# Second FFN output GEMM of a decoder layer with the tokens stationary, in two passes, and its norm per token tile

## The reference

```python
def swiglu(u, w_in, w_out):
    a, b = jnp.split(u @ w_in, 2, axis=-1)
    return (jax.nn.silu(a) * b) @ w_out
...
    h = swiglu(modulate(x, 2), p['w_ffn2_in'], p['w_ffn2_out'])
    x = layer_norm(ALPHA * x + 0.5 * gate[:, 2] * h, p['ln_gain'][2], p['ln_bias'][2])
```

## Time and profile before

| | us |
|---|---|
| median of 3 runs (lowest, highest) | 1374.67 (1374.25, 1376.31) |
| the profiled execution, its own time | 1382.03 |
| span of its trace | 1380.3 |
| mean granted clock of PE over the span | 0.967 |
| PE busy | 1300.8 |
| DVE busy | 564.1 |
| ACT busy | 425.6 |
| POOL busy | 183.5 |

### The profile page before, as it was taken

The page is one execution under the profiler, slowest core; times in us unless marked ns, Lnnn a source line. Parts: engine busy times, 40 slices in busy tenths (PEclk is TensorE's granted clock), DMA queues, the critical chain, the costliest instruction groups (busy, mean ns, idle before and its releaser), DMA issues.

```text
span 1380.3 us, 26475 instructions
## 1 busy us (share of the span) xinstructions
PE 1300.8 (94%) x10178; PEld 1199.9 (87%) x10178; DVE 564.1 (41%) x964; ACT 425.6 (31%) x678; POOL 183.5 (13%) x351
## 2 busy tenths in 40 slices
PE   4999999999999997998979899979999999999996
PEld 3899999999999997996646667979999999999995
DVE  2423222232233357115458766673333233323355
ACT  2222222222211225225446654243222222211123
POOL 3000000000000024552280061032000000000020
PEclk8899999999999998999989999979999999999996
DMA  9544545455444343863740063212222322222211
GB/s 296 162 135 146 158 122 174 130 151 153 132 133 134 109 104 77 194 148 88 229 115 3 2 193 100 82 41 77 84 83 76 91 76 85 78 71 84 84 56 69
DMA packets 253198, 156.08 MB, mean 113 GB/s; under 512 B 46187, under 2 KB 247159, under 8 KB 253063
## 3 DMA queue, kind: packets, MB, share of 16 engines
q1 hardware_dynamic: 247759, 139.83, 36.2%
q0 software_dynamic: 5376, 15.43, 3.8%
HBM read 150.86 MB, written 8.60 MB: 116 GB/s over the span
## 4 chain that ended last, share of the span: by engine, by line
PE 85%; DVE 7%; ACT 4%; issue 2%; DVEq 1%; DMA 1%; SPq 0%; POOL 0%; POOLq 0%; ACTq 0%
PE ps L307 69%; PE ps L776 3%; PE ps L1968 2%; PE ps L785 1%; PE ps L1162 1%; PE ps L284 1%; ACT AR L1383 1%; DVE AR L2001 1%; DVE XT L470 1%; PE ps L1179 1%; PE ps L369 1%; DVEq L469 1%; PE ps L1270 1%; DMA AR<-in_x_sample_dram 1%; DVE UL L353 1%
## 5 line engine op out<-in xcount | busy, mean ns | idle before, releaser
L267 DVE TENSOR_TENSOR WL<-RAW,WH 128x1024 fp32r<-128x1024 f32 x159 | 197.2, 1241 | 408.9 <-ACT WH L263 403.6
L307 PE MATMUL ps<-UH,WH 128*128 128x288 f32 x1680 | 359.9, 295 | 3.1 <-ACT MU L641 1.6
L307 PE MATMUL ps<-UL,WH 128*128 128x288 f32 x1680 | 359.3, 294 | 0.0
L307 PE MATMUL ps<-UH,WL 128*128 128x288 f32 x1680 | 357.9, 294 | 0.0
L307 PEld LDWEIGHTS ps<-UH,WH 128*128 128x128 f32 x1680 | 268.4, 188 | 3.6 <-ACT MU L641 1.8
L307 PEld LDWEIGHTS ps<-UH,WL 128*128 128x128 f32 x1680 | 269.9, 188 | 0.0
L307 PEld LDWEIGHTS ps<-UL,WH 128*128 128x128 f32 x1680 | 268.7, 188 | 0.0
L263 ACT ACTIVATE WH<-RAW 128x1024 fp32r<-128x1024 f32 x159 | 167.2, 1052 | 212.2 <-PE ps L307 202.8
L307 PE MATMUL ps<-HH,WH 128*128 128x288 f32 x704 | 152.6, 298 | 2.9 <-DVE HL L658 2.7
L506 POOL TENSOR_TENSOR AR<-AR 128x576 f32<-128x576 f32 x18 | 29.5, 1640 | 940.3 <-ACT AR L417 877.1
L307 PE MATMUL ps<-HH,WL 128*128 128x288 f32 x704 | 150.8, 295 | 0.0
(11 more groups left out here) (307 smaller groups left out, 1279.1 us busy)
## 6 DMA issues: line engine op xcount, KB each, us to landing
RAW<-in_w_ffn_in_dram SPq DMA_DIRECT2D x88, 512.0 KB, 4.9
AW<-in_w_ada_dram SPq DMA_DIRECT2D x56, 512.0 KB, 4.4
RAW<-in_w_ffn_out_dram SPq DMA_DIRECT2D x32, 448.0 KB, 3.7
RAW<-in_w_ffn_out_dram SPq DMA_DIRECT2D x16, 512.0 KB, 4.0
AR<-in_w_ada_dram SPq DMA_DIRECT2D x7, 1024.0 KB, 10.8
RAW<-in_w_in_dram SPq DMA_DIRECT2D x28, 256.0 KB, 4.0
AR<-in_cache_k_cmp_dram POOLq DMA_DIRECT2D x64, 64.0 KB, 2.6
AR<-in_cache_k_slc_dram SPq DMA_DIRECT2D x64, 64.0 KB, 3.2
```

Of the source, the lines that this page charges most:

```text
L267: nc.vector.tensor_tensor(WL[:, slot, :], RAW[:, slot, :], WH[:, slot, :].bitcast(F32), ALU.subtract).then_inc(split_done, 1)
L307: mm = nc.tensor.matmul(ps[:, 2 * uslot + h, 0:HT], W[:, wslot, k * P:(k + 1) * P], R[:, k0 + k, h * HT:(h + 1) * HT], start=(first and k ...
```

## The change

The output GEMM of the second FFN now has the hidden activations as the stationary operand and the weights as the moving one, so its result has tokens on partitions. The first FFN stays as it was.

- A chunk is one contraction tile, 128 full rows of `w_ffn2_out` (4 KB a row). There are 22, and each is loaded and split twice, once per pass over the tokens: `tokens_sp`, `tokens_hi`, `tokens_lo`, 44 chunks. A third load buffer is used, `AW[:, 1]`.
- The tokens are five units: prompt tiles 0 to 3 of 128 tokens and the 64 sample tokens (unit 4). The first pass does units 0, 4 and 1, the second 2 and 3. A prompt unit takes six matmuls of 512 columns per chunk (three products by two halves of the features), the sample unit four: its high and low parts lie beside each other in `H2` and form one stationary tile of 128, whose two halves of the result are added at the end (`PAIR`).
- In the first pass PE also transposes x from `XT` to rows (`turn_x`, nine fills after chunks 2, 4, ... 18); ACT writes them times ALPHA to `XA`.
- At the pass's last chunk (21) and at the last two (42 and 43) the matmuls go unit by unit. Chunk 42 has none of its own: they are issued with those of chunk 43.
- A unit's norm is along the free axis: DVE multiplies by the gate (`gated`), adds x and sums (`summed`), ACT squares with the mean as bias and sums (`squares_at`) and takes the root, DVE forms `(x + nmean) * gain` (`scaled`) and `* rstd + bias` (`shifted`). For units 0, 1 and 4 this stands between the splits of the second pass, for 2 and 3 at the end. The last steps of unit 2 are shared by ACT, DVE and POOL.
- Gate, gain and bias rows are spread over the partitions by 23 DMAs of POOL at the start of the first pass; the gate row is transposed in the input GEMM (`gate_rows_pe`, `gate_rows_act`) and written to DRAM first.
- The old residual, sums, broadcasts, transposes and copies of the last norm go. SP stores eight pieces instead of ten, the first three before the end.

The core of the diff:

```diff
 PHASES = [("setup", 0, 4, 4), ("ffn1_in", 2 * FT, FT, FT), ("ffn1_out", 3 * KT, 4, 4), ("ln0", 0, 1, 0),
           ("w_in", 15, 8, 7), ("w_out", 8, 4, 4), ("ln1", 0, 1, 0), ("ffn2_in", 2 * FT, FT, FT),
-          ("ffn2_out", 3 * KT, 4, 4), ("ln2", 0, 1, 0), ("y", 0, 3, 2)]
+          ("ffn2_out", 2 * FT, 0, 0)]
...
+        def tokens_sp(sp, w2):
+            n0 = CH0["ffn2_out"]
+            for j in range(2 * FT):
+                dst, full, _count = raw_at(j)
+                sp.wait_ge(split_done, n0 + j + 1 if j < 2 else n0 + j)
+                k = j % FT
+                sp.dma_start(dst, w2[0, k * P:(k + 1) * P, :]).then_inc(full, 16)
+
+        def tokens_hi(act, j):
+            n = CH0["ffn2_out"] + j
+            src, full, count = raw_at(j)
+            act.wait_ge(full, count)
+            if j - 2 == FT - 1:
+                act.wait_ge(tok_mm, len(EARLY))
+            else:
+                act.wait_ge(chunk_mm, n + 1 if j - 2 < FT - 1 else n)
+            nc.scalar.activation(WH[:, n % 2, :], src, ACT.Copy).then_inc(hi_done, 1)
...
+            def part(j, t, q):
+                k, w = j % FT, (n0 + j) % 2
+                W = (WH, WH, WL)[q]
+                if t == 4 and q == 1:
+                    return None
+                if q == 2:
+                    pe.wait_ge(split_done, n0 + j + 3)
+                at = TP if t == 4 else t * P + (T + TS if q == 1 else 0)
+                src = H2[:, k, at:at + P]
+                for h in range(2):
+                    out = ps[:, OBANK[t][h] if t < 4 else h, :]
+                    mm = nc.tensor.matmul(out, src, W[:, w, h * 512:(h + 1) * 512], start=(k == 0 and q == 0),
+                                          stop=(k == FT - 1 and q == 2))
+                return mm
...
+            for j in range(2 * FT):
+                k, units = j % FT, (EARLY, LATE)[j // FT]
+                pe.wait_ge(hi_done, n0 + j + 1)
+                if j < FT:
+                    pe.wait_ge(hl_done, FT + 2 + k)
...
+                if j < 2 * FT - 2 and k < FT - 1:
+                    for q in range(3):
+                        for t in units:
...
+                            mm = part(j, t, q)
+                    mm.then_inc(chunk_mm, 1)
+                elif k == FT - 1 and j < FT:
...
+                elif k == FT - 1:
+                    for t in units:
+                        for c in (j - 1, j):
+                            for q in range(3):
+                                mm = part(c, t, q)
+                        mm.then_inc(tok_mm, 1)
...
+        def tokens_dve(dve):
...
+            gated(dve, 3)
+            summed(dve, 3)
+            for h in range(2):
+                gated(dve, 4, h)
+            rstd_at(dve, 3, 4)
+            nc.vector.tensor_tensor(NMR, NMT[:, 2:3], RST[:, 2:3], ALU.mult).then_inc(nmr_ready, 1)
+            summed(dve, 4)
+            nc.vector.drain()
+            scaled(nc.vector, 4)
+            rstd_at(dve, 4, 5)
+            for h in range(2):
+                shifted(nc.vector, 4, h)
+            dve.wait_ge(xn_done, 1)
+            nc.vector.tensor_tensor(y2(1), y2(1), b2("gain", 1), ALU.mult)
+            nc.vector.drain()
+            nc.vector.tensor_tensor(y2(1), y2(1), b2("bias", 1), ALU.add).then_inc(y_done, 1)
```

More of the change, by code:

```diff
@@ L472, in ln_dve @@
                         center(m + 2)
-                if mod is not None and m >= 1:
+                if m >= 1:
                     mod_lo(dve, m - 1, mod)
@@ L479, in ln_act @@
             nc.scalar.activation(SDV, VAR, ACT.Sqrt, bias=EPSC[0:TT, :]).then_inc(sd_ready, 1)
-            if mod is not None:
-                hi(act, *split_args(AFTER[mod], 1))
+            hi(act, *split_args(AFTER[mod], 1))
             for m in range(KT):
                 act.wait_ge(normed, KT * i + m + 1)
[L484 to L491, removed]
                 if m >= 2:
@@ L559, in in_body @@
                         first_pair(pe, a, KT * 3)
+                    if i == 2 and first and j == 1:
+                        gate_rows_pe(pe)
                     if i == 1:
@@ L691, in ffn_dve @@
             dve.sem_inc(stat_in, 1)
[L692 removed]
+            it, q = KT // 2 - 1, 0
             for j in range(6):
@@ new lines, in build @@
+        OBANK = {0: (4, 5), 1: (6, 7), 4: (4, 4), 2: (2, 3), 3: (0, 1)}
+        XA = AR2[:, 0:KT * T]
+        BC = carve(AR2[:, KT * T:AR2N], KT * T, [("gate", D), ("gain", D), ("bias", D), ("gate_s", 512), ("gain_s", 512),
+                                                 ("bias_s", 512)])
+        GROWS = nc.dram_tensor("gate_rows_dram", [NC, D], F32, kind="Internal").ap()
+        NMT, SUMT, SQT, SDT, RST = (MU[:, 8 * q:8 * q + 5] for q in range(5))
+        NMR = MU[:, 40:41]
+        TMP = T2[:, :, :].rearrange("p a n -> p (a n)")
@@ new lines, in gated @@
+        def gated(dve, u, h=None):
+            t = UNITS[u]
+            n = 2 if t < 4 else 1
+            if not h:
+                nc.vector.drain()
+            if u != 1:
+                dve.wait_ge(tok_mm, u + 1)
+            out, src, g = (TMP[:, 0:n * 512].rearrange("p (h n) -> p h n", h=n), obanks(t),
+                           spread_row("gate", t).rearrange("p (h n) -> p h n", h=n))
+            if h is not None:
+                out, src, g = out[:, h], src[:, h], g[:, h]
+            nc.vector.tensor_tensor(out, src, g, ALU.mult).then_inc(tok_read, 1)
@@ new lines, in summed, with mean_at @@
+        def summed(dve, u):
+            t = UNITS[u]
+            nc.vector.drain()
+            x = unit(XA, t)
+            z = nc.vector.tensor_tensor_reduce(out=x, in0=TMP[:, 0:x.shape[1]], in1=x, scale=1.0, scalar=0.0, op0=ALU.add, op1=ALU.add,
+                                               accum_out=SUMT[:, t:t + 1])
+            if t == 4:
+                z.then_inc(sum_s, 1)
+                return
+            nc.vector.drain()
+            mean_at(u, SUMT[:, t:t + 1])
+        def mean_at(u, src):
+            t = UNITS[u]
+            nc.vector.tensor_scalar(NMT[:, t:t + 1], src, -1.0 / D, None, ALU.mult).then_inc(nm_ready, 1)
@@ new lines, in rstd_at, with quarters, ytile, scaled @@
+        def rstd_at(dve, u, count):
+            t = UNITS[u]
+            dve.wait_ge(sdt_ready, count)
+            nc.vector.reciprocal(RST[:, t:t + 1], SDT[:, t:t + 1])
+            nc.vector.drain()
+        def quarters(ap):
+            return ap.rearrange("p (k n) -> p k n", n=256)
+        def ytile(t):
+            if t not in (2, 3):
+                return quarters(unit(XA, t))
+            return early_columns(4 * (t - 1))
+        def scaled(eng, u):
+            t = UNITS[u]
+            eng.scalar_tensor_tensor(out=ytile(t), in0=quarters(unit(XA, t)), scalar=NMT[:, t:t + 1],
+                                     in1=quarters(spread_row("gain", t)), op0=ALU.add, op1=ALU.mult)
@@ new lines, in shifted, with y2, b2 @@
+        def shifted(eng, u, h=None):
+            t = UNITS[u]
+            x, b = ytile(t), quarters(spread_row("bias", t))
+            if h is not None:
+                x, b = x[:, 2 * h:2 * h + 2, :], b[:, 2 * h:2 * h + 2, :]
+            eng.scalar_tensor_tensor(out=x, in0=x, scalar=RST[:, t:t + 1], in1=b, op0=ALU.mult,
+                                     op1=ALU.add).then_inc(y_done, 1)
+        def y2(h):
+            return ytile(2)[:, 2 * h:2 * h + 2, :]
+        def b2(name, h):
+            return quarters(BC[name])[:, 2 * h:2 * h + 2, :]
@@ L756, in build, with tail_pool @@
+        def tail_pool(pool):
+            pool.wait_ge(xn_done, 1)
+            nc.gpsimd.tensor_tensor(y2(0), y2(0), b2("gain", 0), ALU.mult)
+            pool.drain()
+            nc.gpsimd.tensor_tensor(y2(0), y2(0), b2("bias", 0), ALU.add).then_inc(y_pool, 1)
         wav = w_ada[0].rearrange("(k p) n -> p k n", p=P)
```

318 lines of the change are left out of this document (232 added, 86 removed).

## The result

| | before | changed |
|---|---|---|
| median, us (lowest, highest; 8 runs each) | 1376.07 (1374.18, 1380.81) | 1368.08 (1364.85, 1371.37) |
| profiled execution, its own time | 1382.03 | 1366.22 |
| span of its trace | 1380.3 | 1364.6 |
| from one pace behind the last input matmul's start, to the end of the last output matmul | 146.9 | 152.7 |
| from there to the span's end | 28.75 | 13.1 |

The ratio of the times is 0.993, with a 95% interval of 0.9913 to 0.9947: faster by 9.6 us (7.3 to 12.0). The forecast was 17.2, and 1357.5 us for the time (1354 to 1361, over its cases 1350.5 to 1365): the median of 1368.1 lies outside.

The account below looks back on a forecast made before the run. TensorE, busy 94% of the span, and the serial tail behind it were taken as the bound; 0.8 us from the GEMM plus 16.45 from the tail, 17.2 off 1374.67, gave 1357.5 (1354 to 1361; over the cases 1350.5 to 1365).

Parts of the forecast that it names:

- the size of a wide matmul: Output GEMM of the second FFN: 616 matmuls of 512 columns at 225 ns each, 138.6 us (131.4 to 144.1).
- the upper bound of 234: Output GEMM: a 512-column matmul's time if the whole 131.7 ns of a 288-column one scales with the columns.
- the plain float32 row: Profile row of 14 plain float32 matmuls, read as 255 ns each, 15 over 240; taken to set excess per matmul.
- Rival (a): Output GEMM: no excess on a wide matmul, 216 ns each, TensorE ends 5.6 us earlier, 1351.9 us; chance 0.14.
- The small matmuls: Output GEMM: 32 transposes 3.8, 8 plain half-width matmuls 0.6, pair sums 0.6, together 5.0 us; 1.0 more unplaced.
- The stall: Output GEMM, before the last two chunks: TensorE waits 1.35 us for chunk 43's high part, with no lower clock charged.
- The wait of 2.69 us and the clock behind it: Start of the output GEMM: TensorE's wait for the last HL piece and the lower clock after it both go.
- The tail: After TensorE's last matmul: 12.3 us to the end instead of 28.75, a gain of 16.45.
- is hidden: Tail: GpSimd's half of tile 2's gain and bias, 2 x 1.06 us from T + 3.9, claimed to be covered.
- (b): Second pass: norm work between splits makes TensorE wait, 1 us at each of seven insertions, 1364.5 us; chance 0.13.
- (c): Second-pass weight loads set the pace and the kernel gets slower, 1415 us at a landing of 10.8; chance 0.05.

## Why the prediction was wrong, and where it was right

**The failed step is the size of a wide matmul.** "I take 213.3 + 11.7 = 225 ns" put the excess on the matmul. It goes with the columns: 233.4 ns at 512, at the upper bound of 234 that the prediction had worked out and not taken. This is 616 x 8.4 ns = 5.2 us of the 7.6 that the gain fell short.

The argument for it was the plain float32 row, 255 ns apart for 240 of columns, so "the excess goes with the matmul". That row was misread. Its 14 starts include two that came late; the nine behind them are even (timeline of the kernel before, window 806.6 to 812):

```profile
806.41 2.35 PE L1298 MATMUL ps<-AR 128*128 128x288 f32 x9
```

(2.35 - 0.41)/8 = 242.5 ns, where the columns streamed twice are 240: 2.5 over, and not 15. At the same width the reduced type has 12.2 over its 120. Read so, the row speaks against a cost of each matmul and shows the excess to be the type's own.

The runs show, for this type, 0.456 to 0.460 ns a column at three widths (with one exception, the 0.443 at half width), the same with zero activations, and next to none of the excess with 2-byte parts. At 1.2 GHz rows 3 show none with 4-byte parts either (240 ns for 288 columns), and the prediction had read that as a per-matmul cost that hides. A limit of some 0.45 ns a column explains both this (0.833 a column there) and the plain float32 row (0.842), which are slower anyway. That last step is an argument; no run changed the clock, and the 0.443 says that such a limit would not be a fixed number.

Seen this way the new GEMM had to lose: it streams 315,392 columns instead of 304,128, 3.7% more at nearly one price per column. Rival (a) would have been true of 2-byte parts, and is the wrong side of the truth here.

**The small matmuls: 5.0 + 1.0 against 7.3.** The 32 transposes came out near their price, 3.5 for 3.8. The sample's fill, the join of its halves and its sums took 3.3 instead of 1.2. The trace has two records for each plain float32 matmul (the join is two matmuls in the program and x4 in the rows above, L1298 is 8 and x16), so the "8 of 512 columns in 1.92 us" were four matmuls, and fill and join were priced at half. Besides, the two halves of the fill ran mostly one behind the other (16 records from 1225.95 to 1227.26), and the four matmuls of the sums (0.6) had no term.

**The stall: 1.35 forecast, 1.46 measured**, in the place named, and taken out by the experiment with a buffer of its own. The clock stayed at 1.00 through it, as assumed.

**The wait of 2.69 us and the clock behind it: right.** Both are gone, and alone they are worth 4.5 us of GEMM (4.2 forecast).

**The tail: 12.3 forecast, 13.1 measured.** The steps came within some 0.3 us, most on the short side, but for the two beside GpSimd. The prediction allowed 0.3 for them from rows 9; they took 0.74 and 1.06 longer than alone (0.3 of the first is covered: without it VectorE waits 0.29 for the root), and the experiment without GpSimd brings the tail to 12.3. That this is the forecast's number is luck: VectorE does two operations more there than the forecast had, and the last store needs less than the changed kernel's. It also shows that "is hidden" was true of the end of GpSimd's half and not of its effect.

**Rivals (b) and (c)** did not come about: the second pass has no wait but the one, and a load lands in 3.4 us. With 2-byte parts one chunk, the last, waited for its load.

**The sum.** Gains: tail 15.65, wait and clock 4.35. Losses: 4.2 for more columns (143.8 against 1056 x 0.1322 = 139.6), 1.6 for stall and drains, and 4.3 for small matmuls (7.3 now, where the sums between the products and what could not be placed made 2.95). 20.0 - 10.1 = 9.9 by the traces, 9.6 by the times.

## What to carry to other kernels

Price a matmul by its columns at the pace that the same operand type shows in the trace, and take a per-instruction excess only if two widths of that type show it; where both bounds can be worked out from rows, an argument from another type is too weak to choose the lower. Read a pace from starts that stand evenly, without the first ones behind a wait, and count matmuls in the program: a record is not always one. Turning a GEMM round pays by what follows it (norm along the free axis, no transposes, a tile finished while the next one multiplies), not by wider matmuls. In a serial tail, check what an engine that "helps for free" does to the operations beside it.

## What was not expected of the hardware

- 4-byte reduced-float matmuls run at 0.456 ns a column at the 2.4 GHz level, 9.5% over the clock's 0.417; 2-byte ones at 216 ns for 512 and 122.5 for 288. Which of the two operands has to be 2-byte was not tried.
- Of 256 columns such matmuls stood 117.8 ns apart for the first 20 us and 113.4 for the next 120, at the same granted clock. The cause is open.
- A plain float32 matmul leaves two records, each 242.5 ns behind the one before at 288 columns.
- A weight load's record takes 98 ns with 2-byte parts and 188 with 4-byte ones. It is not what sets the pace: 256-column matmuls 113.4 ns apart ran over such loads of 4 bytes.
- A VectorE operation of 512 columns took 1.75 us instead of 0.69 beside GpSimd's, and GpSimd's own 1.64 instead of 1.06 (rows 7): both sides pay.
- TensorE kept its clock over waits of 1.3 to 1.6 us and lost it behind one of 2.69, in the kernel before and again in its 2-byte form.
